# Even blocks, joined attention slots, and an eighth weight slot in a four-layer hybrid trunk

## What is computed

```
for layer in range(4):
    h = rms_norm(x, norm_w[layer])
    if kind == 0:   # HGRN2, 8 heads of 128
        q, f, v, g = split(h @ w_in, 4)
        # chunkwise recurrence: scores within blocks with decays, plus a carried state
        y = (rms_norm(o, o_norm_w) * silu(g)) @ w_out
    elif kind == 1: # attention, 16 heads of 64, three groups (window, dilation)
        # (128, 1), (512, 4), (2048, 16): q and k normed, ALiBi, softmax
        o = sum over groups of softmax(lse over groups)[g] * o[g]
        y = (o * silu(g)) @ w_out
    else:           # gMLP: gelu(u) * (causal 128x128 mix of layer_norm(gelu(v))) * silu(g)
        y = (...) @ w_out
    x = x + y
```

## Time and profile before

| | |
|---|---|
| median of 3 runs | 1381.55 us (1380.89 to 1382.06) |
| the profiled execution, its own time | 1381.57 us |
| its span in the trace | 1379.4 us |
| PE busy | 1370.8 us, 99% |
| DVE, ACT, POOL busy | 942.3, 691.1, 92.5 us |
| granted PE clock | 1.0 throughout |

### The profile page before, as it was taken

The page is one execution under the profiler, slowest core; times in us unless marked ns, Lnnn a source line. Parts: engine busy times, 40 slices in busy tenths (PEclk is TensorE's granted clock), DMA queues, the critical chain, the costliest instruction groups (busy, mean ns, idle before and its releaser), DMA issues.

```text
span 1379.4 us, 23267 instructions
## 1 busy us (share of the span) xinstructions
PE 1370.8 (99%) x9311; PEld 1147.6 (83%) x9311; DVE 942.3 (68%) x1666; ACT 691.1 (50%) x1211; POOL 92.5 (7%) x128
## 2 busy tenths in 40 slices
PE   9999999999999999999999999999999999999999
PEld 8888887898887878788878777799888988888878
DVE  7677778673667676667667676767657467777782
ACT  6444545353646465656565566464434344454450
POOL 2111212000000000000000000000000012111110
PEclk9999999999999999999999999999999999999999
DMA  6322233332222222222222221323333322232311
GB/s 189 93 77 77 62 88 98 99 93 76 77 77 77 77 77 77 77 76 77 77 77 77 67 62 56 98 73 92 95 89 92 107 78 76 62 92 77 88 52 61
DMA packets 211693, 113.69 MB, mean 82 GB/s; under 512 B 3744, under 2 KB 209890, under 8 KB 211587
## 3 DMA queue, kind: packets, MB, share of 16 engines
q1 hardware_dynamic: 211202, 112.02, 28.2%
q0 software_dynamic: 384, 0.20, 0.1%
HBM read 110.10 MB, written 2.10 MB: 81 GB/s over the span
## 4 chain that ended last, share of the span: by engine, by line
PE 94%; DVE 2%; ACT 2%; issue 1%; DMA 0%; SPq 0%; ACTq 0%; DVEq 0%
PE ps L594 38%; PE ps L609 37%; PE scores L609 4%; PE scores L977 2%; PE ps L1008 2%; PE ps L991 2%; PE scores L779 2%; PE ps L957 2%; PE ps L808 1%; PE ps L623 1%; PE ps L810 1%; PE scores L797 1%; PE scores L755 1%; DVE w_lo L1695 1%; PE ps L819 1%
## 5 line engine op out<-in xcount | busy, mean ns | idle before, releaser
L609 PE MATMUL ps<-w_hi,op_hi 128*128 128x512 f32 (+1 forms) x880 | 320.3, 364 | 3.5 <-DVE op_lo L1753 1.8
L594 PE MATMUL ps<-op_hi,w_hi 128*128 128x512 f32 (+1 forms) x800 | 317.8, 397 | 0.0
L609 PE MATMUL ps<-w_lo,op_hi 128*128 128x512 f32 (+1 forms) x880 | 309.5, 352 | 0.0
L609 PE MATMUL ps<-w_hi,op_lo 128*128 128x512 f32 (+1 forms) x880 | 308.8, 351 | 0.0
L594 PE MATMUL ps<-op_lo,w_hi 128*128 128x512 f32 (+1 forms) x800 | 305.5, 382 | 0.0
L594 PE MATMUL ps<-op_hi,w_lo 128*128 128x512 f32 (+1 forms) x800 | 304.9, 381 | 0.0
L1695 DVE TENSOR_TENSOR w_lo<-raw,w_hi 128x1024 fp32r<-128x1024 f32 x200 | 240.8, 1227 | 37.3 <-ACT w_hi L1198 36.7
L1198 ACT ACTIVATE w_hi<-raw 128x1024 fp32r<-128x1024 f32 x200 | 202.8, 1051 | 37.4 <-PE ps L609 13.0
L609 PEld LDWEIGHTS ps<-w_hi,op_hi 128*128 128x128 f32 x880 | 166.6, 189 | 29.1 <-issue 6.4
L609 PEld LDWEIGHTS ps<-w_lo,op_hi 128*128 128x128 f32 x880 | 166.4, 189 | 23.0
L609 PEld LDWEIGHTS ps<-w_hi,op_lo 128*128 128x128 f32 x880 | 166.9, 190 | 18.7 <-issue 0.2
(11 more groups left out here) (215 smaller groups left out, 1813.2 us busy)
## 6 DMA issues: line engine op xcount, KB each, us to landing
raw<-in_b_w_in SPq DMA_DIRECT2D x80, 512.0 KB, 3.9
raw<-in_a_w_in SPq DMA_DIRECT2D x64, 512.0 KB, 4.2
raw<-in_c_w_in SPq DMA_DIRECT2D x24, 512.0 KB, 4.8
raw<-in_a_w_out SPq DMA_DIRECT2D x16, 512.0 KB, 4.1
raw<-in_b_w_out SPq DMA_DIRECT2D x8, 512.0 KB, 4.0
raw<-in_c_w_out SPq DMA_DIRECT2D x8, 512.0 KB, 4.6
xt<-in_x SPq DMA_DIRECT2D x4, 512.0 KB, 6.2
y<-in_norm_w SPq DMA_DIRECT2D x3, 512.0 KB, 4.3
```

Of the source, the lines that this page charges most:

```text
L594: last = nc.tensor.matmul(bank, a, b, start=(k == 0 and p == 0), stop=(k == KT - 1 and p == 2))
L609: last = nc.tensor.matmul(bank, a, b, start=(k == 0 and p == 0), stop=(k == KT - 1 and p == 2))
```

## The change

It does five things.

1. `w_hi` and `w_lo` get an eighth slot (the `scratch` tensor shrinks from 17072 to 15024 columns; some attention tiles share places). The output projection's last four chunks then fit, and its eight units of 256 columns become four of 512. In the last layer the last tile stays in two halves. Chunk 7 is split before the residual adds and not after the fifth.
2. The first two weight chunks of the next layer are requested by SP ahead of the norm weights.
3. The widest HGRN2 visit deals its twelve blocks over the four partition groups so that each gets 192 columns; `keep_blocks` becomes five copies instead of three.
4. The attention scores of slots 1 and 3 go to other banks, slot 1 to `obank` and `spare`, slot 3 to the `turn` banks. The visits are now: scores 0 and 1 after step 4; `turn_p` alone after 15, 25, 39 and 49; scores 2, 3 and values 0, 1 after 28; values 2, 3 after 53. `turn_p(2)` waits until slot 3 has been biased, since that frees the `turn` banks.
5. ACT's and DVE's plans follow, and the last mix is reordered by hand.

```diff
-HALF = 3
-SLOTS = 2 * HALF + 1
+HALF = 4
+SLOTS = 2 * HALF
-NARROW = ((0, 0), (0, 1), (1, 0), (1, 1), (0, 2), (1, 2), (0, 3), (1, 3))
-OUT_UNITS = WIDE + len(NARROW)
+OUT_UNITS = 2 * WIDE
+BLOCKS_OF = (((0, 0), (1, 0)), ((2, 0), (3, 0)), ((0, 1), (1, 1), (2, 1)), ((3, 1), (0, 2), (1, 2), (2, 2), (3, 2)))
-SLOT_AT = (4, 15, 26, 38, 50, 62)
+SCORES_AT = (4, 28)
+BIAS_AT = (4.5, 14.5, 28.5, 33.5)
+EXPS_AT = (8.5, 18.5, 32.5, 38.5)
+NORMAL_AT = (10.4, 22.1, 36.1, 44.1)
+TURN_AT = (15, 25, 39, 49)
+VALUES_AT = (28, 53)
...
+        slot_banks = (score, (obank, spare), score, turn)
...
                     def scores(w):
-                        if w or later:
-                            pe.wait_ge(s_biased, h * B_SLOTS + w)
+                        if w == 1 and later:
+                            pe.wait_ge(mg_sub, h)
+                            pe.wait_ge(t_copied, h)
+                        if w == 2:
+                            pe.wait_ge(s_biased, h * B_SLOTS + 1)
+                        if w == 3:
+                            pe.wait_ge(pT_act, h * B_SLOTS + 2)
+                            pe.wait_ge(pT_dve, h * B_SLOTS + 2)
...
                     def turn_p(w):
                         pe.wait_ge(p_done, h * B_SLOTS + (w + 1))
+                        if w == 2:
+                            pe.wait_ge(s_biased, h * B_SLOTS + B_SLOTS)
...
                     if mix and not proj:
                         scores(0)
+                        scores(1)
                         turn_qk(2)
                         turn_qk(3)
                         first_half(0)
                         turn_qk(4)
-                        scores(1)
                         turn_qk(5)
...
                         turn_p(1)
                         values(0)
                         scores(3)
+                        values(1)
                         first_half(5)
-                        values(1)
                         turn_p(2)
                         second_half(0)
-                        values(2)
...
                         turn_lse()
+                        values(2)
                         values(3)
...
                         for w in range(B_SLOTS):
-                            plan.append((SLOT_AT[w] + 0.5, lambda w=w: bias(w)))
-                            plan.append((SLOT_AT[w] + 0.6, lambda w=w: peak(w)))
-                            plan.append((SLOT_AT[w] + (6.4 if w == 0 else 8), lambda w=w: normalise(w)))
-                            plan.append((SLOT_AT[w + 1] + 0.9, lambda w=w: p_out(w)))
+                            plan.append((BIAS_AT[w], lambda w=w: bias(w)))
+                            plan.append((BIAS_AT[w] + 0.1, lambda w=w: peak(w)))
+                            plan.append((NORMAL_AT[w], lambda w=w: normalise(w)))
+                            plan.append((TURN_AT[w] + 0.9, lambda w=w: p_out(w)))
```

More of the change, by code:

```diff
@@ L489, in load_columns, with load_first @@
                     load((n0 + c) % RAW, columns(w, col), n0 + c)
+            def load_first(n, chunks):
+                for c in chunks:
+                    w, col = ((a_w_in[n // 3], A_PARTS[c] * D) if n % 3 == 0 else
+                              (b_w_in[0], B_PARTS[c] * D) if n == 1 else (c_w_in[0], D + c * P))
+                    load((IN0[n] + c) % RAW, columns(w, col), IN0[n] + c)
             def load_layer(n, w, parts):
@@ L768, in quad_scores @@
                             pe.wait_ge(sd_done, h * KEPT + (2, 5)[r - 1])
+                        if m == WINDOW:
+                            ends = [0] * WINDOWS
+                            for group, n in BLOCK_ORDER:
+                                t, w = BLOCKS_OF[group][n]
+                                keys = slice(t * P + w * m, t * P + (w + 1) * m)
+                                start, wide = ends[group], (3 - w) * m
+                                ends[group] += wide
+                                last = nc.tensor.matmul(bank[group * m:(group + 1) * m, start:start + wide],
+                                                        a_k[:, prev, keys],
+                                                        a_qq[:, prev, 0:3 - w, keys.start + m:keys.stop + m],
+                                                        start=True, stop=True)
+                                if n + 1 == len(BLOCKS_OF[group]):
+                                    last.then_inc(g_ready, 1)
+                            return
                         for t in range(TT):
-                            for w in range(WINDOWS if m < WINDOW else WINDOWS - 1):
+                            for w in range(WINDOWS):
                                 rows = slice(w * WINDOW, (w + 1) * WINDOW)
                                 keys = slice(t * P + w * WINDOW, t * P + (w + 1) * WINDOW)
[L773 to L778, removed]
+                                of = a_qq[:, prev, 0:2, keys].rearrange("p x (h c) -> p x h c", c=4 * m)[:, :, :, m:]
+                                to = bank[rows, t * 48:t * 48 + 48]
                                 last = nc.tensor.matmul(to, a_k[:, prev, keys], of, start=True, stop=True)
@@ L1342, in keep_blocks @@
                         act.wait_ge(g_ready, h * G_STEPS + G_STEPS)
-                        for w in range(WINDOWS - 1):
-                            keys = slice(w * WINDOW, (w + 1) * WINDOW)
-                            of = score[1][keys, 0:384].rearrange("p (t c) -> p t c", t=TT)[:, :, 0:(3 - w) * WINDOW]
-                            last = nc.scalar.activation(a_sd[keys, :, keys.stop:], of, ACT.Copy)
+                        for group, tiles, w, at in ((0, slice(0, 2), 0, 0), (1, slice(2, 4), 0, 0), (2, slice(0, 3), 1, 0),
+                                                    (3, slice(3, 4), 1, 0), (3, slice(0, 4), 2, 64)):
+                            wide, count = (3 - w) * WINDOW, tiles.stop - tiles.start
+                            of = score[1][group * WINDOW:(group + 1) * WINDOW, at:at + count * wide]
+                            last = nc.scalar.activation(a_sd[w * WINDOW:(w + 1) * WINDOW, tiles, (w + 1) * WINDOW:],
+                                                        of.rearrange("p (t c) -> p t c", t=count), ACT.Copy)
                         last.then_inc(sd_spread, 1)
@@ L1460, in p_out @@
                         act.wait_ge(pT_ready, h * 8 + (2 * w + 1))
-                        if w or later:
-                            act.wait_ge(bo_ready, h * B_SLOTS + w)
+                        if w > 1 or w == 0 and later:
+                            act.wait_ge(bo_ready, h * B_SLOTS + w - 1)
                         first = keys_from(w)
-                        nc.scalar.activation(b_pt[:, 0, first:], turn[0][:, first:], ACT.Copy).then_inc(pT_act, 1)
+                        nc.scalar.activation(b_p[w][:, 0, first:], turn[0][:, first:], ACT.Copy).then_inc(pT_act, 1)
                     def log_sums():
```

148 lines of the change are left out of this document (83 added, 65 removed).

## The result

The changed kernel takes 1406.75 us (median of 4 runs, 1405.48 to 1407.55), the kernel before 1381.61: a ratio of 1.018, 95% interval 1.016 to 1.020. I had forecast 1392.6, in a range of 1385 to 1403. The sign was right; the time lies 14 us above the forecast and 4 above the range.

What follows compares the result with a forecast made beforehand. The PE's instruction stream was taken as the bound. Terms of -4.3, +0.1, -4.8, -7.7, +3.9, +22.4 and +1.4 summed to +11.0 on 1381.6, giving 1392.6 us, with an eight-in-ten range of 1385 to 1403.

Steps and rivals of the forecast that it cites:

- output projection: 720 matmuls of 256 columns become 360 of 512: -4.3 us, with 0.1 us put on what hides the rest.
- widest visit: Widest HGRN2 visit, dealt evenly, takes the 8-token visit's 0.67 us instead of 0.97, in 16 visits: -4.8 us.
- joined slots: Attention heads: fewer entries and turns between matmul shapes save 1.1 us a head over seven passes: -7.7 us.
- turn_p(1): PE waits 0.55 us a head, as DVE's and ACT's 14.2 us chain outlasts the PE's 13.6: +3.9 us.
- turn_p(2): After step 39 the PE waits 3.1 us a head for DVE's normalise(2), plus 0.9 in the seventh pass: +22.4 us.
- last mix: scores(3) waits for DVE's p_out(1), so bias(3), normalise(2) and turn_p(2) come about 1.5 us later: +1.4 us.
- What bounds the kernel, and how an instruction is priced: The PE's instruction stream is the kernel; each PE instruction costs the distance between starts.
- Savings: Output projection -4.3 us, evenly dealt widest HGRN2 visit -4.8 us, joined attention slots -7.7 us.
- the savings don't come: Rival: the even deal gains nothing and joined attention slots save half, giving 1401 us; chance 0.10.
- The two deadlines: New PE waits in each attention head, at turn_p(1) for +3.9 us and at turn_p(2) for +22.4 us.
- the pauses don't come: Rival: DVE has peak(3) and normalise(2) done in time, leaving only the savings, 1366 us; chance 0.08.
- the clock falls in the pauses: Rival: seven attention-head pauses each bring a half-speed PE stretch, 7 x 3 = 21 us, giving 1414 us; chance 0.10.

Runs made afterwards that it cites:

- narrow_out: bias3_early with each of the fifteen 512-column output projection units issued as two runs of 256 columns: 1382.90 us.
- deal_only: The kernel before with nothing but the even deal of the widest HGRN2 visit: 1376.98 us, ratio 0.9965.
- best: bias3_early with turn_p(1) one step later, turn_p(2) two later, and the last mix's p_out(1) ahead of peak(2) on DVE: 1369.93 us, ratio 0.9915.
- best2: best with DVE's unit(1) ahead of p_out(0): 1367.05 us, ratio 0.9901.
- fill6: The changed kernel with 6 extra unused matmuls on the PE ahead of each of the seven waits for turn_p(2): 1396.19 us.
- bias3_early: The changed kernel with bias(3) and peak(3) ahead of unit(3) on DVE instead of ahead of normalise(2): 1379.19 us, ratio 0.998.
- fill13: The changed kernel with 13 extra unused matmuls on the PE ahead of each of the seven waits for turn_p(2): 1395.97 us, ratio 1.010.
- turn2_late: The changed kernel with turn_p(2) and the two p_out(2) behind it moved from step 39 to step 44: 1384.35 us, ratio 1.002.
- fill3: The changed kernel with only 3 extra unused matmuls on the PE ahead of turn_p(2)'s wait: 1400.27 us (one run).

## Why the prediction was wrong

By its own steps, in us (spans of the traces; +26.3 is to be explained):

| step | forecast | measured | read from |
|---|---|---|---|
| output projection | -4.2 | -4.4 | stretches of narrow_out |
| widest visit | -4.8 | -4.4 | deal_only |
| joined slots | -7.7 | -7.6 | visits of a head without waits: 16.4 before, 15.3 in best |
| turn_p(1) | +3.9 | +3.1 | 7 x 0.44 |
| turn_p(2) | +22.4 | +23.1 | 7 x 3.2, and 0.7 in the seventh head |
| last mix | +1.4 | +1.7 | last turn_qk to the next layer |
| unit(1) | 0 | +2.9 | 7 x 0.42, best2 |
| clock | 0 | +12.1 | heads of the changed kernel against fill6 |
| sum | +11.0 | +26.5 | |

The rows add up to the difference of the spans within 0.2 us. (The prediction's own line on turn_p(2), 7 x 3.1 + 0.9, is 22.6 and not 22.4; nothing hangs on it.)

*What bounds the kernel, and how an instruction is priced:* right. Every term of the forecast that was made from distances of starts came within 0.8 us.

*Savings:* right, all three, the first two by a kernel with that part alone or undone, the joined slots only by the lengths of the visits. The rival "the savings don't come" is out.

*The two deadlines:* right in place, and in size at turn_p(2), where the chain is the one that the earlier trace rows gave: 3.2 us against 3.1. Around turn_p(1) the sum is 2.1 us short, as told below. The rival "the pauses don't come" is out. In the way that I wrote it, bias(3) and peak(3) ahead of normalise(2) on DVE, it also named the cure: bias3_early moves these two into DVE's idle 2.49 us and gains 27.6.

*The step that failed: the weight of the rival "the clock falls in the pauses".* I had its mechanism, its place and a time (1414), and gave it 0.10, put the clock at nothing in the sum and left it out of the range. No row stands behind that: the earlier trace rows show no wait above 1.2 us, so the trace of before couldn't speak on a pause of 3.1 in either direction, as the prediction says itself; and the forecast pause was 2.6 times as long as the longest that it had shown. A forecast that puts seven pauses of a new length into a stream has to treat the clock at its upper level as an open term, with an end on each side: at nothing and at 7 x 3 = 21 us. Had I done so, the range would have reached past 1410. With fill6 the term is 12.1 us, between them. The rival was right in kind and too dear: in five of the seven heads the low stretch lasted about as long as one pause and not two, and in the seventh it cost nearly nothing.

*A smaller step, mis-sized: the PE's way to turn_p(1), with unit(1) on it.* I compared DVE's deadlines at the two turn_p only. The projection's own bank hand-over, DVE's unit(1) against the PE's fourth bank, had lost its room too. The visit after step 15, between the second bank's end and the fourth bank, had shrunk from 1.87 to 0.66 us, since scores(1) had left it, while DVE's work there was the same: a wait of 0.42 us a head. In the changed kernel this wait adds nothing of its own, because turn_p(1) behind it starts only when DVE's chain is done. The chain is as long as forecast (14.2 us from turn_qk(6)), and it sets the same start in best2, where the wait for unit(1) is gone and turn_p(1) stands one step later. The changed kernel, then best2, second head:

```profile
429.95 0.60 PE L997 MATMUL ps<-ident,scratch 128*128 128x128 f32 x4
...
444.17 1.09 PE L1041 MATMUL ps<-ident,scratch 128*128 128x128 f32 x8 [0.21 <-DVE scratch L2230]
...
423.45 0.60 PE L997 MATMUL ps<-ident,scratch 128*128 128x128 f32 x4
...
437.67 1.09 PE L1041 MATMUL ps<-ident,scratch 128*128 128x128 f32 x8
```

Both are 14.22 us. Without the first wait the second would be longer by as much. So the two rows of the table belong together: 6.0 us where I had 3.9, since the PE needs 14.22 - 0.44 - 0.42 = 13.4 us for its own work on this way and not 13.6. With this and the clock the forecast would have been 1392.6 + 2.1 + 12.1 = 1406.8, at a measured 1406.75. That it fits so closely is luck: the other rows miss by 1.3 us together, and the medians differ by 1.2 us less than the spans.

*Still open:* what decides whether a pause of 2.3 us lowers the clock. The program alone doesn't. The wait of 2.2 us for scores(3) in the last mix stands in seven of these kernels; in the profiled executions the clock fell behind it in fill13, fill6, bias3_early and turn2_late, and not in the changed kernel, fill3 and narrow_out, and bias3_early's ten executions are of both kinds. It was not tried whether less or more work ahead of a pause matters.

## What to carry to other kernels

When an edit takes work out of the engine that bounds a kernel, list every result that this engine waits for within one period, bank hand-overs too, and compare each with the PE's new place, not only those that the diff names. When a forecast pause of TensorE is longer than any that the profile shows, its price can be more than its length; put the clock's part into the sum with both ends, or fill the pause with throw-away matmuls, which here gained 10.8 us. Look for the idle time of the engine that is late: a late chain with a hole ahead of it wants another order and not less work.

## What the runs showed of the hardware that I had not expected

- The same pause, behind the same work, lowered the clock in four heads and not in three (2.32 us by the waits); 1.64 us never did and 3.00 always did, in seven heads each. The low stretch behind a pause cost 1.5 to 1.6 us, 2.8 where two followed each other, and 0.3 where another engine was late behind it. Executions of one kernel differ in whether it comes at all.
- A page that reads 9 in all its 40 clock slices can hide seven drops, 12 us in all: 0.98 over a head is what one of them looks like.
- A wait of 0.16 us in the waits row cost the PE's stream 0.40 to 0.42 us by the distances of starts.
- Twenty-one microseconds of added matmuls in a pause cost nothing: fill13 and fill6, with 13 and 6 of them a head, differ by 0.2 us.
